# Places of ScalarE and VectorE steps in the mixer stage of a hybrid encoder layer on Trainium2

## Chip, cores and metric

One core of one Trainium2 chip runs the whole program. The metric is device time in microseconds (us), the median of several executions. The hardware profiler gives one further execution with the start and duration of every instruction. Engines are called PE (TensorE matmul), PEld (its weight load), ACT (ScalarE), DVE (VectorE), POOL (GpSimd) and SP (SyncE); POOL and SP issue transfers here.

## What is computed

One layer of a streaming encoder: a macaron feed-forward block, a mixer with two parallel branches, a second feed-forward block, a final norm. 512 prompt tokens and 8 x 16 sample tokens go through it, 640 columns in all. The change concerns the mixer:

```python
def conformer_conv_branch(glu_in, conv_buf, w_dw, b_dw, ln_g, ln_b, w_pw):
    u = glu_in[..., :D_CONV] * jax.nn.sigmoid(glu_in[..., D_CONV:])
    v, new_buf = causal_depthwise_conv(u, conv_buf, w_dw, b_dw)      # width 31
    ...
def mamba2_branch(z, xbc, dt_raw, conv_buf, ssm_state, w_conv, b_conv, dt_bias, a_log, d_skip, norm_g, w_out):
    xbc_c, new_buf = causal_depthwise_conv(xbc, conv_buf, w_conv, b_conv)   # width 4
    xbc_c = jax.nn.silu(xbc_c)
    ...
    dt = jax.nn.softplus(dt_raw.astype(f32) + dt_bias.astype(f32))
    A = -jnp.exp(a_log.astype(f32))
    y, h_fin = ssd_scan(xh, dt, A, Bm, Cm, ssm_state)
    y = (y + d_skip.astype(f32)[:, None] * xh.astype(f32)).reshape(b, L, D_INNER)
    g = (y * jax.nn.silu(z.astype(f32))).reshape(b, L, N_GROUPS, D_INNER // N_GROUPS)
    g = g * lax.rsqrt(jnp.mean(g * g, axis=-1, keepdims=True) + RMS_EPS)
    g = g.reshape(b, L, D_INNER) * norm_g.astype(f32)
    return g.astype(z.dtype) @ w_out, new_buf, h_fin.astype(z.dtype)
```

## The kernel before

**Tiling.** Activations lie transposed, 128 channels by 640 tokens. A matmul in fp32 precision is made of three fp32r products: weights and activations are both split into a high and a low part. A *job* is one block of 128 output channels: 48 matmuls (8 input blocks, three products, two halves of 320 columns), or 24 where the input has 4 blocks. ACT casts a job's raw weights to the high part (`split_hi`, L520), DVE subtracts to get the low part (`split_lo`, L979). There are two weight buffers and two output banks, so job j+2's high part may be written only after job j has ended on PE, and job j+2 starts only once job j's bank has been read out (`evac_done`).

**Order.** Every engine has one queue, and the order in it is the order in which the source writes it; waits are on semaphores, and what is queued behind a wait stands still.

**The mixer.** Four groups (g = 0 to 3) run one after another, each with GJ = 22 jobs, k = 0 to 21. NX = 6 jobs (k = 0 to 5) give x, B and C. Of each, ACT copies the bank into a padded tile and starts the width-4 convolution (`xbc_in`, L762 to L770, five instructions), DVE adds three taps (`conv_xbc`, L1372), ACT applies SiLU (`xbc_silu`, L783) and the D skip (`skip`, L776). k = 6 and 7 are a gate and a value of the conformer branch (J_U0), k = 8 to 11 are z, k = 12 and 13 a second gate and value (J_U1). Five SSD tiles of 128 tokens follow jobs 7 to 11 on PE: in the middle of each of these jobs PE turns x and B (`turn(t)`, L1776 to L1778), at its end it multiplies (`tile(t)`: L1791, L1798, L1804). Tile t needs the decay matrix: ACT takes exponentials of broadcast cumulative sums that POOL's queue fetched from DRAM (`decay(t)`, L799 to L805, `decay_h(t)`, L810), DVE multiplies (`prepare(t)`, L1411). k = 14 to 21 (from J_O) are the output projection, 24 matmuls each, scaled on DVE by the group norm's reciprocal root, which comes from a sum over tokens (L1642), a variance (L995), Ln and Exp on ACT (`inverse_root`, L534 and L536) and three Newton steps on DVE (L1001 to L1005). `sample_state` (L1448) and PE's `sample(b)` (L1836) are the sample tokens' states.

**The width-31 convolution** has 30 taps per channel block on DVE (`conv_glu`, L1344), two blocks c = 0, 1 a group. The table `TAPS` says after which k how many are done; keys from GJ on fall into the next group. Before its first tap ACT copies the block with its halo (`long_conv_in`, L736 to L740) and POOL's queue fetches the sample halo (L449) once the other block's last tap is done.

**Only in group 0** are dt and the cumulative sums made (`dt_stage` on ACT, L709 to L725, and on DVE, L1297 to L1327; `cumulate` on PE, L1751 to L1754). POOL sends the sums to DRAM and fetches them back in broadcast form (`acb`, L464).

## Time and profile before

| | |
|---|---|
| median of 3 runs | 1857.89 us (1857.85 to 1858.5) |
| profiled execution | 1861.42 us, its span 1859.6 us |
| PE busy | 1770.9 us, 95% |
| DVE, ACT, POOL busy | 70%, 47%, 5% |
| mean granted TensorE clock | 0.981 of full speed |
| longest waits of PE, by who ended them | `w_lo` L979 20.3 us in 13 waits; `xa_lo` L1010 9.7 in 1 (at the start); L1791, put down to issue, 9.1 in 4; `h_pr` L1399 4.2 in 3; `ext_b` L764 4.1 in 1; dt's L1322 3.2 in 1 |

The numbers of the profiled execution go with its own time, which lies 3.5 us above the median. "Busy" is the share of the span in which an engine has an instruction in work. The granted clock has two levels in this trace, full (2.4 GHz) and half (1.2 GHz).

### The profile page before, as it was taken

To read this page: it belongs to the slowest core of one execution; us is meant where nothing else is said; L and a number is where in the kernel's file an instruction comes from. 1 tells how busy PE (TensorE), PEld (TensorE's weight loads), DVE (VectorE), ACT (ScalarE), POOL (GpSimd) and SP (SyncE) were. 2 spreads that over 40 slices of the span, in tenths; PEclk is the share of its full clock that TensorE was granted. 3 is DMA by queue.
4 is the path that set the end of the run, shared out by engine and by line. 5 is a ranking of instruction groups with operands and counts; after the bars stand their busy time and mean duration, and the time that the engine had idled before them with its cause. 6 is when DMAs were issued, how large, how long until landed. Compare 5 with 4: busy or idle time off the path is not lost.

```text
span 1859.6 us, 28933 instructions
## 1 busy us (share of the span) xinstructions
PE 1770.9 (95%) x11823; PEld 1712.9 (92%) x11823; DVE 1305.7 (70%) x1626; ACT 870.1 (47%) x1473; POOL 95.4 (5%) x149
## 2 busy tenths in 40 slices
PE   7999999999899999998999899998999999999996
PEld 7999999999888898898889888998999999999995
DVE  6963873776739789879887998775556854863764
ACT  5431441444767357726754773255234432441432
POOL 0000000000011101010201100010000000000000
PEclk9999999999989999999999999999999999999998
DMA  4222212214142344153325423232222212222212
GB/s 157 82 73 84 91 69 91 91 62 142 53 141 77 117 121 137 50 163 100 102 74 148 113 70 125 76 131 68 69 76 73 81 67 91 91 69 91 91 44 81
DMA packets 49714, 173.62 MB, mean 93 GB/s; under 512 B 6800, under 2 KB 6960, under 8 KB 45232
## 3 DMA queue, kind: packets, MB, share of 16 engines
q1 hardware_dynamic: 39024, 137.41, 22.5%
q0 software_dynamic: 10560, 34.38, 6.3%
q8 instruction: 94, 1.54, 0.3%
q14 instruction: 36, 0.29, 0.1%
HBM read 155.56 MB, written 16.20 MB: 92 GB/s over the span
## 4 chain that ended last, share of the span: by engine, by line
PE 78%; DVE 11%; ACT 6%; issue 4%; DMA 1%; ACTq 0%; DVEq 0%; SPq 0%; POOLq 0%
PE ps L1615 48%; PE ps L1676 23%; DVE v L1344 4%; DVE pair L1372 2%; PE ps L1633 2%; DVE w_lo L979 1%; PE ps L1836 1%; ACT w_hi L520 1%; DMA ext_a<-in_halo_a 1%; PE ps L1791 1%; PE ps L1642 1%; ACT acb L802 1%; PE ps L1798 1%; PE ps L1804 1%; PE ps L1825 0%
## 5 line engine op out<-in xcount | busy, mean ns | idle before, releaser
L1615 PE MATMUL ps<-xa_hi,w_hi 128*128 128x320 f32 x1504 | 363.8, 323 | 19.0 <-DVE w_lo L979 11.2
L1615 PE MATMUL ps<-xa_lo,w_hi 128*128 128x320 f32 x1504 | 345.2, 311 | 0.0
L1615 PE MATMUL ps<-xa_hi,w_lo 128*128 128x320 f32 x1504 | 345.2, 311 | 0.0
L520 ACT CAST w_hi<-w_raw 128x1024 fp32r<-128x1024 f32 (+2 forms) x188 | 178.7, 951 | 277.1 <-PE ps L1615 240.2
L1676 PE MATMUL ps<-t_hi,w_hi 128*128 128x320 f32 x952 | 297.0, 312 | 11.5 <-issue 11.5
L1615 PEld LDWEIGHTS ps<-xa_hi,w_hi 128*128 128x128 f32 x1504 | 254.0, 190 | 46.8 <-issue 27.9
L1676 PE MATMUL ps<-t_lo,w_hi 128*128 128x320 f32 x952 | 296.4, 311 | 0.0
L1676 PE MATMUL ps<-t_hi,w_lo 128*128 128x320 f32 x952 | 296.2, 311 | 0.0
L979 DVE TENSOR_TENSOR w_lo<-w_raw,w_hi 128x1024 fp32r<-128x1024 f32 (+2 forms) x188 | 208.2, 1108 | 88.6 <-ACT w_hi L520 86.7
L1615 PEld LDWEIGHTS ps<-xa_lo,w_hi 128*128 128x128 f32 x1504 | 254.1, 190 | 0.0
L1615 PEld LDWEIGHTS ps<-xa_hi,w_lo 128*128 128x128 f32 x1504 | 253.9, 190 | 0.0
L1344 DVE SCALAR_TENSOR_TENSOR v<-ext_a,par,v 128x640 f32<-128x640 f32 x240 | 211.9, 883 | 11.5 <-DMA ext_a<-in_halo_a 5.3
L1676 PEld LDWEIGHTS ps<-t_hi,w_hi 128*128 128x128 f32 x952 | 180.7, 190 | 12.9 <-issue 12.9
L1676 PEld LDWEIGHTS ps<-t_lo,w_hi 128*128 128x128 f32 x952 | 180.7, 190 | 0.0
L1676 PEld LDWEIGHTS ps<-t_hi,w_lo 128*128 128x128 f32 x952 | 180.7, 190 | 0.0
L1615 PE MATMUL ps<-h_hi,w_hi 128*128 128x320 f32 x704 | 160.4, 309 | 0.0
L1615 PE MATMUL ps<-h_hi,w_lo 128*128 128x320 f32 x704 | 160.4, 309 | 0.0
L1615 PE MATMUL ps<-h_lo,w_hi 128*128 128x320 f32 x704 | 160.4, 309 | 0.0
L1231 DVE SCALAR_TENSOR_TENSOR x<-ps,x 128x640 f32<-128x640 f32 x48 | 39.6, 825 | 153.9 <-PE ps L1615 153.5
L1615 PEld LDWEIGHTS ps<-h_lo,w_hi 128*128 128x128 f32 x704 | 117.7, 188 | 0.0
L1615 PEld LDWEIGHTS ps<-h_hi,w_hi 128*128 128x128 f32 x704 | 117.7, 188 | 0.0
L1615 PEld LDWEIGHTS ps<-h_hi,w_lo 128*128 128x128 f32 x704 | 117.7, 188 | 0.0
(264 smaller groups left out, 2619.9 us busy)
## 6 DMA issues: line engine op xcount, KB each, us to landing
w_raw<-in_w_mix SPq DMA_DIRECT2D x56, 512.0 KB, 3.8
raw_b<-in_w_sp SPq DMA_DIRECT2D x18, 1024.0 KB, 4.8
w_raw<-in_w_sp SPq DMA_DIRECT2D x16, 1024.0 KB, 4.8
w_raw<-in_w_down SPq DMA_DIRECT2D x32, 512.0 KB, 3.7
w_raw<-in_w_tail SPq DMA_DIRECT2D x32, 512.0 KB, 3.7
w_raw<-in_w_gu SPq DMA_DIRECT2D x20, 512.0 KB, 3.8
acb<-cum_dram POOLq DMA_DIRECT2D x20, 512.0 KB, 7.3
w_raw<-in_w_ssm SPq DMA_DIRECT2D x32, 256.0 KB, 2.7
```

The lines of the kernel that those rows point to most:

```text
L520: nc.scalar.copy(hi, w_raw[:, b, 0:width]).then_inc(hi_done, 1)
L802: nc.scalar.activation(acb[:, s, j], acb[:, s, j], ACT.Relu, scale=-1.0, bias=tokg[:, 1, t, j:j + 1]).then_inc(dec_step, 1)
L979: nc.vector.tensor_tensor(lo, w_raw[:, b, 0:width], hi.bitcast(F32), ALU.subtract).then_inc(lo_done, 1)
L1231: nc.vector.scalar_tensor_tensor(xc, job_out(b), 0.5, xc, ALU.mult, ALU.add).then_inc(evac_done[b], 1)
L1344: nc.vector.scalar_tensor_tensor(out, ext_a[:, :, j:j + TS], par[:, g, w0 + j:w0 + j + 1], out, ALU.mult, ALU.add).then_inc(conva_ready[c] ...
L1372: nc.vector.scalar_tensor_tensor(out, ext_b[:, s, :, j:j + TS], param(w0 + j), out, ALU.mult, ALU.add).then_inc(tap_b if j < taps - 1 else ...
L1615: last = nc.tensor.matmul(psj[:, b, u, 0:TH], w[:, cols], act_in[:, k, u * TH:(u + 1) * TH], start=(k == 0 and n == 0), stop=(k == chunks ...
L1633: last = nc.tensor.matmul(psj[:, b, u, 0:TH], w[:, b, cols], act_in[:, k, u * TH:(u + 1) * TH], start=(k == 0 and n == 0), stop=(k == chun ...
L1642: last = nc.tensor.matmul(pab[:, u, 0:TH], const[:, ONES], acc[:, u * TH:(u + 1) * TH], start=True, stop=True)
L1676: last = nc.tensor.matmul(ps[:, sp_set(n) + BANK[q], 0:TH], w[:, k * P:(k + 1) * P], t[:, X_OF[q], k * TH:(k + 1) * TH], start=(first and ...
L1791: last = nc.tensor.matmul(pc[e * PD:(e + 1) * PD, c * P:(c + 1) * P], xdt[:, hh * PD:(hh + 1) * PD], mdec[:, hh], start=True, stop=True)
L1798: last = nc.tensor.matmul(pd[:, c * P:(c + 1) * P], h_pr[:, c * P:(c + 1) * P], bc[:, 1, cols], start=True, stop=True)
```

## The change

Five orders change, and the numbers of taps. No instruction is made larger or smaller.

- `inverse_root` of the group norm stands before `next_hi(J_O)` on ACT. On DVE the low split for job 16 stands right behind the read-out of job 14 and no longer behind the sum, sample state and tap that follow it.
- In groups 1 to 3, the halo copies of the previous group's block c = 1 (`long_conv_in(1, g - 1)`) stand behind the high split of job 3 and no longer ahead of it.
- In groups 1 to 3, `tokg`'s copy, `decay(0)` and `decay_h(0)` stand behind `skip(2)` in k = 4 and no longer behind the gate's sigmoid in k = 6.
- In group 0, `dt_stage` on ACT stands behind `xbc_in`, `xbc_silu` and `skip` of its k; on DVE dt's first sum (k = 2) is done at k = 0. `cumulate` on PE and the copies behind it are at k = 6, not 5.
- Taps of c = 0 in the SSD tiles: 4, 3, 3, 3 for 5, 4, 4, 4; block J_O loses its tap; the last job of the group has 2 for 1, the next group's k = 0 has 6 for 4, k = 1 has 3 for 1. Taps of c = 1: 5 for 4 at k = 2, 5 for 6 at 7.5.

```diff
-TAPS = ({8.5: 5, 9.5: 4, 10.5: 4, 11.5: 4} | {k: 1 for k in range(J_O, GJ)} | {GJ: 4, GJ + 1: 1},
-        {GJ + 2: 4, GJ + 3: 4, GJ + 4: 4, GJ + 5: 5, GJ + 6: 7, GJ + 7.5: 6})
+TAPS = ({8.5: 4, 9.5: 3, 10.5: 3, 11.5: 3} | {k: 1 for k in range(J_O + 1, GJ - 1)} | {GJ - 1: 2, GJ: 6, GJ + 1: 3},
+        {GJ + 2: 5, GJ + 3: 4, GJ + 4: 4, GJ + 5: 5, GJ + 6: 7, GJ + 7.5: 5})
...
-                if k == 5:
+                if k == NX:
                     act.wait_ge(cum_mm, 1)
...
+                def scales():
+                    nc.scalar.copy(tokg[:].rearrange("p a t h -> p (a t) h"),
...
                     if k > 3 or not dt_stage:
                         next_hi(k)
-                    if dt_stage:
-                        dt_stage(k)
+                    if k == 2 and g:
+                        long_conv_in(1, g - 1)
                     xbc_in(k)
...
-                    if k == 1 and g:
-                        long_conv_in(1, g - 1)
+                    if dt_stage:
+                        dt_stage(k)
+                    elif k == NX - 2:
+                        scales()
+                        decay(0)
+                        decay_h(0)
...
                 next_hi(J_U1 + 1)
+                inverse_root(N_GROUP + g, 2 + g)
                 next_hi(J_O)
-                inverse_root(N_GROUP + g, 2 + g)
                 next_hi(J_O + 1)
...
-                    if k > 3 or carried:
+                    if (k > 3 or carried) and k != J_O + 1:
                         split_lo(*at(k + 1), KM * P if k + 1 < J_O or k + 1 == GJ else GC * P)
...
-                    else:
+                    elif k != 2:
                         dt_stage(k)
+                    if not carried and k == 0:
+                        dt_stage(2)
...
+                            if c == 0:
+                                split_lo(*at(k + 2), GC * P)
                             evacuated(k)
...
-                        if k == 5 and first:
+                        if k == NX and first:
                             cumulate()
```

ACT in group 0, k = 1 to 3. `xs<-pair` is a SiLU, `pair<-ps` to `new_b<-ext_b` are one `xbc_in`, `dts` are dt's steps.

```order
 L783 ACT_TABLE_LOAD
+L783 ACTIVATE xs<-pair 128x640
+L762 ACTIVATE pair<-ps,parg 128x640
+L764 COPY ext_b<-ps 128x40x16
+L766 COPY ext_b<-halo_b 128x8x3
+L769 COPY ext_b<-ext_b 128x31x3
+L770 COPY new_b<-ext_b 128x27
 L783 ACTIVATE xs<-pair 128x640
 L709 ACTIVATE dts<-dts 128x160
```

The whole `xbc_in` of job 2 and the SiLU of job 1 now stand ahead of dt's first step on ACT.

ACT in groups 1 to 3, k = 4 to 5. The first `CAST` behind these rows is the high part of job 6.

```order
+L783 ACTIVATE xs<-pair 128x640
+L776 ACTIVATE y<-xs,parg 128x640
+L836 COPY tokg<-tok 128x120
+L799 ACT_TABLE_LOAD
+L799 ACTIVATE el<-acb 128x8
+L802 ACTIVATE acb<-acb,tokg 128x128 x8
+L805 ACTIVATE acb<-acb 128x1024
+L810 ACTIVATE ach<-ach 128x512
+L520 CAST w_hi<-w_raw 128x1024
```

Before, the cast followed the `skip` (L776) directly. Two table loads a group come on top, since the SiLUs on both sides need another table.

DVE in group 1 from the norm's variance on, before and then after (line numbers are each kernel's own). `w_lo` ahead of `rstd<-pair` is job 15's, the next one job 16's.

```order
L1448 TENSOR_TENSOR z<-z,ps 128x512
L979 TENSOR_TENSOR w_lo<-w_raw,w_hi 128x512
L1001 SCALAR_TENSOR_TENSOR rstd<-pair 128x640
L1003 TENSOR_TENSOR rstd<-rstd,pair 128x640
L1005 SCALAR_TENSOR_TENSOR rstd<-rstd,pair 128x640
L1509 TENSOR_TENSOR y<-ps,rstd 128x640
L1512 TENSOR_TENSOR yb<-yb,y 128x640
L1448 TENSOR_TENSOR z<-z,ps 128x512
L1344 SCALAR_TENSOR_TENSOR v<-ext_a,par,v 128x640
L979 TENSOR_TENSOR w_lo<-w_raw,w_hi 128x512
```

```order
L986 TENSOR_TENSOR w_lo<-w_raw,w_hi 128x512
L1008 SCALAR_TENSOR_TENSOR rstd<-pair 128x640
L1010 TENSOR_TENSOR rstd<-rstd,pair 128x640
L1012 SCALAR_TENSOR_TENSOR rstd<-rstd,pair 128x640
L1518 TENSOR_TENSOR y<-ps,rstd 128x640
L986 TENSOR_TENSOR w_lo<-w_raw,w_hi 128x512
L1523 TENSOR_TENSOR yb<-yb,y 128x640
```

Job 16's low part has moved ahead of three instructions, and one tap there is gone.

## Rows read from the trace of the kernel before

**Rows 1.** Waits of PE over the span: in all, times, longest.

```profile
PE ps L1615 <- DVE w_lo L979: 20.3, 13, 3.9
```

**Rows 2.** Timeline of PE, group 0: start us, us, instruction, [idle before, releaser].

```profile
500.37 0.87 PE L1615 MATMUL ps<-xa_hi,w_hi 128*128 128x320 f32 x2 [4.07 <-ACT ext_b L764]
...
512.15 0.41 PE L1751 MATMUL ps<-dts,const 128*128 128x32 f32 x2 [3.15 <-DVE dts L1322]
...
546.22 1.10 PE L1791 MATMUL ps<-mdec,xdt 128*64 128x128 f32 x16 [2.96 <-issue]
```

**Rows 3.** Timeline of ACT, group 0.

```profile
493.90 0.74 ACT L783 ACTIVATE xs<-pair 128x640 f32<-128x640 f32 x1
496.75 0.34 ACT L709 ACTIVATE dts<-dts 128x160 f32<-128x160 f32 x1 [2.11 <-DVE dts L1301]
...
508.86 1.02 ACT L520 CAST w_hi<-w_raw 128x1024 fp32r<-128x1024 f32 x1
```

**Rows 4.** POOL's timeline in group 0, and landing of line L464's transfers.

```profile
522.78 0.94 POOL L464 DMA_DIRECT2D acb<-cum_dram  x1 [2.08 <-DMA cum_dram<-cum_sb]
...
DMA to landing us min/median/max: 4.8/7.3/8.7
```

**Rows 5.** Chain of work that ended last: start us, us, what.

```profile
518.92 9.49 PE ps L1615 x48
...
549.51 4.31 PE ps L1615 x24
...
789.63 5.32 PE ps L1615 x24
795.82 3.52 PE ps L1615 x24
...
899.87 4.87 PE ps L1615 x24
```

**Rows 6.** Timeline of PE, group 1 and (898.67) group 2.

```profile
670.81 0.55 PE L1615 MATMUL ps<-xa_hi,w_hi 128*128 128x320 f32 x2 [1.76 <-DVE w_lo L979]
...
711.16 1.61 PE L1791 MATMUL ps<-mdec,xdt 128*64 128x128 f32 x16 [2.03 <-issue]
...
789.63 0.56 PE L1615 MATMUL ps<-gn_hi,w_hi 128*128 128x320 f32 x2 [2.48 <-DVE w_lo L979]
...
898.67 0.66 PE L1776 MATMUL ps<-const,xs 128*128 128x128 f32 x4 [1.87 <-DVE h_pr L1399]
```

**Rows 7.** Timeline of ACT, group 1, k = 2 to 7.

```profile
668.46 1.03 ACT L520 CAST w_hi<-w_raw 128x1024 fp32r<-128x1024 f32 x1
...
685.48 0.89 ACT L762 ACTIVATE pair<-ps,parg 128x640 f32<-128x640 f32 x1 [3.09 <-PE ps L1615]
...
688.68 1.04 ACT L520 CAST w_hi<-w_raw 128x1024 fp32r<-128x1024 f32 x1
...
704.71 1.28 ACT L799 ACT_TABLE_LOAD   x1
...
710.23 0.25 ACT L832 COPY btok<-ps 128x128 f32<-128x128 f32 x1
```

**Rows 8.** Timeline of DVE, group 1, k = 5 to 7.

```profile
691.53 1.22 DVE L979 TENSOR_TENSOR w_lo<-w_raw,w_hi 128x1024 fp32r<-128x1024 f32 x1
692.66 4.56 DVE L1344 SCALAR_TENSOR_TENSOR v<-ext_a,par,v 128x640 f32<-128x640 f32 x5
...
709.84 1.22 DVE L1411 TENSOR_TENSOR mdec<-acb,cbm 128x1024 f32<-128x1024 f32 x1 [0.59 <-ACT acb L805]
```

**Rows 9.** Timelines of DVE and ACT, group 1, k = 13 to 15.

```profile
777.62 0.82 DVE L995 TENSOR_SCALAR pair<-ps 128x640 f32<-128x640 f32 x1 [0.42 <-PE ps L1642]
...
783.32 0.83 DVE L1001 SCALAR_TENSOR_TENSOR rstd<-pair 128x640 f32<-128x640 f32 x1 [2.34 <-ACT pair L536]
...
788.89 0.69 DVE L979 TENSOR_TENSOR w_lo<-w_raw,w_hi 128x512 fp32r<-128x512 f32 x1
...
782.47 0.74 ACT L536 ACTIVATE pair<-pair 128x640 f32<-128x640 f32 x1
```

More of the change, by code:

```diff
@@ L832, in btok_out @@
                     nc.scalar.copy(btok[:], pb[:, 0:NS]).then_inc(btok_ready, 1)
+                def scales():
+                    nc.scalar.copy(tokg[:].rearrange("p a t h -> p (a t) h"),
+                                   tok[:].rearrange("p a t h -> p (a t) h")[:, :, bass.ds(g * HG, HG)]
+                                   ).then_inc(tokg_ready, 1)
+                    act.wait_ge(tokg_ready, g + 1)
                 if not dt_stage:
@@ L857, in group @@
                     dt_stage(NX)
-                nc.scalar.copy(tokg[:].rearrange("p a t h -> p (a t) h"),
-                               tok[:].rearrange("p a t h -> p (a t) h")[:, :, bass.ds(g * HG, HG)]
-                               ).then_inc(tokg_ready, 1)
-                act.wait_ge(tokg_ready, g + 1)
-                if dt_stage:
+                    scales()
                     act.wait_ge(cum_out, 16)
@@ L866, in group @@
                 next_hi(J_U0 + 1)
-                decay(0)
-                decay_h(0)
+                if dt_stage:
+                    decay(0)
+                    decay_h(0)
                 btok_out(0)
@@ L1515, in group @@
                                                     ALU.mult).then_inc(evac_done[b], 1)
+                            if c == 0:
+                                split_lo(*at(k + 2), GC * P)
                         if c < NB - 2:
```

## Prediction, made before the changed kernel ran

> **What bounds the kernel now.** I read the busy shares first (PE 95%), then who ended PE's waits, then the timelines around each wait. PE is the bound, so only its idle time and the time it spends at half clock can be won. The biggest entry is the low weight parts, 20.3 us in 13 waits [rows 1]. In the mixer the timelines place the waits like this. Group 0 stands still before job 4 for 4.07 us (the bank of job 2 has not been copied out), before `cumulate` for 3.15 and before tile 0 for 2.96 [rows 2]. Each of groups 1 to 3 has the same pattern: 1.76 before job 3, 2.03 before tile 0, up to 1.87 in the middle of job 9 (turn 2), and 2.48 before job 16 [rows 6]. An idle stretch often costs twice, since the granted clock falls to half behind it. Job 16 takes 5.32 us where the next job of 24 matmuls takes 3.52; a half job behind turn 2 of group 2 takes 4.87, and one behind tile 0 of group 0 takes 4.31; job 5 behind `cumulate` takes 9.49 where 48 matmuls at full clock take 7.04 [rows 5]. Everything outside the mixer keeps its order, and I cost it at nothing.
>
> I work in the profiled execution's own time (1861.42 us, span 1859.6, 1.8 us around it) and subtract the sum from the median shown, 1857.89, which lies 3.5 lower.
>
> **1. The norm's root and job 16's split (groups 1 to 3).** The variance ends at 777.62 + 0.82 = 778.44, but Exp starts only at 782.47, because Ln stood behind job 15's cast, which waits for job 13, and paid its table load after that [rows 9]. Now Ln's table load waits for nothing and lies ahead of the variance. Ln runs at 778.45 (0.74), a table load (1.28 [rows 7]) and Exp (0.74) end at 781.2. Job 15's cast and low part (about 0.65 each) follow, so DVE's first Newton step starts at 782.4, 0.9 earlier. Three steps and the read-out of job 14 at 0.83 each give 785.7 [rows 9], and job 16's low part, now next, ends at 786.4. Before it started at 788.89 [rows 9]. PE is through with the work ahead of job 16 at 787.15, which is 789.63 less 2.48 [rows 6] (0.2 earlier by the spacing of later jobs, as each sample product overlaps). So the 2.48 wait goes. Job 15 may start 0.3 later, since its cast now stands behind the root. The half clock behind the wait goes too: 5.32 - 3.52 = 1.80 [rows 5]. **Gain 2.48 + 1.80 - 0.3 = 4.0 a group, 12.0 in three.** Late next is job 17's low part, whose cast stands behind job 14's two neighbours and 16 small sample copies on ACT; by the same spacings it is ready at about 791.3, when PE is done with job 16 and its sample product, so up to 0.5 may be lost. The Newton steps overwrite a tile that still leaves for DRAM; they start 0.9 earlier than before, and that transfer could become the wait; bounds 0 and 0.9. Group 0 has the same pattern without a marked half clock; I put its gain at 1.6, the nearest row being its own wait of that kind in [rows 1], bounds 0.5 and 2.5.
>
> **2. Halo copies behind job 3's cast.** The cast at 668.46 [rows 7] moves ahead of 2.5 us of copies, and job 3 starts without its 1.76 wait. But DVE is the bound in k = 2 to 6: from 670.8 on it has no pause, and every job there is released by a low part that comes at the end of a k. What counts is when DVE starts its taps of k = 2. These need the copies, which end at about 669.5, and the sample halo. Before they began 1.1 later, behind the low part; now they begin 1.1 earlier but are 5 for 4, and a tap costs 4.56 / 5 = 0.91 [rows 8]. **Gain 0.2 a group; the 1.76 wait reappears before job 4.** Bounds: -1 (the halo, fetched once the two added taps of k = 1 are done, comes late) and +0.4. I take 0.2.
>
> **3. First decay in k = 4 (groups 1 to 3): a loss.** It takes 710.23 - 704.71 = 5.52 us with its table load [rows 7], plus 0.3 for `tokg`. Behind it now stands job 6's cast. Job 4's `xbc_in`, a SiLU and a skip take 688.68 - 685.48 = 3.20 [rows 7], so the cast starts at 685.25 + 3.20 + 5.82 = 694.3 and ends at 695.3, and DVE's low part for job 6 waits for that; before it ran at 691.53 [rows 8]. DVE stands still for 3.8 us, PE before job 6 for about 4.3, and this is on the path, as DVE is the bound from there to tile 0: 711.16 - 691.53 = 19.6 us of work in a row [rows 6, 8]. What comes back is the 0.59 that the decay product waited for its exponentials [rows 8]. **Loss 3.8 - 0.6 = 3.2 a group, 9.6 in three.** PE's half clock after the 4.3 us wait (1.7 us) is hidden, because job 7 waits for DVE anyway; if it lasts twice as long, about 1 us shows. Bounds of the loss: 2.0 (all of the 2.03 before tile 0 [rows 6] comes back, 3.8 - 1.8) and 5.5 (half clock shows in full, 3.8 + 1.7).
> On the table loads first the row: 1.28 us, and the decay's first exponential starts right behind it, so two more a group are in the sum at 1.28 where they are on the path (one of them; the SiLU's stands in ACT's slack). The Trainium skill, page "ScalarE: Activation LUTs", section "What ACT_TABLE_LOAD costs", puts a switch at 2.66 us, the load and a drain of 1.38. By that rule the loss would be 1.4 larger a group, 4.1 in all, and the sum 15.1 for 19.2, a time of 1842.8. The rows show no such drain, so I leave it out.
>
> **4. Fewer taps in the SSD tiles.** From tile 0 to turn 2, DVE does 6 + 5 taps around the halo fetch; now 5 + 4, that is 1.8 us less on the chain that ended the wait of 1.87 [rows 6]. **Gain 1.7 in group 1, 1.7 + 1.35 (4.87 - 3.52, the half clock [rows 5]) in group 2, 1.6 in group 3: 6.4.** Bounds 3 and 7. The taps that move to the last job, k = 0 and k = 1 lie in DVE's pauses there and cost nothing; if the pause in k = 1 is shorter than I read, 0.9 a group. The tap-free tiles behind turn 2 were bound by PE and gain nothing.
>
> **5. dt's steps in group 0.** ACT waited for dt's first sum until 496.75 and copied job 2's bank only then [rows 3]. Now the sum is made at k = 0, and `xbc_in` of job 2 follows the SiLU of 493.90 directly, at 494.6; the bank is free at 496.1, when job 3 ends (500.37 - 4.07 = 496.3 [rows 2]). So the 4.07 goes. From 496.75 to 508.86 ACT works without a pause, 12.1 us; the same pieces in the new order need one table load less, 10.8, so job 5's cast starts at 494.6 + 10.8 = 505.4 for 508.86 [rows 3] and its low part ends at 507.6. Job 4 ends at 496.3 + 7.04 = 503.4: **a new wait of 4.2 before job 5** takes the place of the old one. `cumulate` then finds dt ready, so 3.15 goes [rows 2]. Job 5, with 1.7 of half clock, ends at 507.6 + 7.05 + 1.7 = 516.4; `cumulate` took 518.92 - 512.15 = 6.8, mostly at half clock [rows 2, 5]; at full clock 4.5. Job 6 then takes 7.04 to 9.49 [rows 5]. With 4.5 and 9.1 it ends at 530, for 535.3 before; with 6.8 and 9.49 at 532.7. ACT is free then, while before it was 2.7 late with the gate's sigmoid. Sigmoid, job 8's cast, table load and exponentials bring the decay to 536.9, PE ends job 7 at 530 + 8.3 = 538.3, and tile 0 starts there for 546.22 [rows 2]. The exponentials also need the broadcast sums: `cumulate` ends at 521, the copies at 522.6, the transfer to DRAM takes some 2.9 (2.08 of it POOL's wait), and the fetch 7.3 (up to 8.7) [rows 4]: 532.8 to 534.2, just when ACT wants them, at 533.0. **Gain 7.9, bounds 4.5 and 8.5**; plus 0.8 (4.31 - 3.52 [rows 5]) as no wait stands before tile 0. I take the upper part of the range since both halves of the chain, PE's and ACT's, meet there.
>
> **The sum:** 12.0 + 1.6 + 0.6 - 9.6 + 6.4 + 8.7 = 19.7, less 0.5 for job 17: 19.2. 1861.4 - 19.2 = 1842.2 profiled, 1857.9 - 19.2 = **1838.7**.
>
> **Rivals.**
> - *The decay costs its upper bound and the clock takes the rest.* Part 3 at 5.5 a group (16.5), part 5 at 5, part 4 at 3: 13.6 - 16.5 + 0.6 + 3 + 5 - 0.5 = 5.2 to about 12 with one of the three at its middle. Time 1846 to 1853. For it: the clock stayed at half through `cumulate` and into job 5. Against: nothing, except that DVE hides one half clock.
> - *The root's order brings nothing*, because job 15's cast behind the root, or job 17's behind the sample copies, becomes the wait: 12 less, 1850.7. Against: PE has 3.9 to 4.4 us a job there, and DVE's work a job is shorter.
> - *Slower:* the decay ahead of job 6's cast. PE waits 4.3 us, then again before job 7 and tile 0, and stays at half clock over all three. The point is reached when the loss is over 11 us a group for my 3.2, that is, 15 us at half clock on the path (7.5) on top of 3.8: 1857.9 - 28.8 + 34 = 1863. For it: a row of waits in group 0 did hold the clock low from tile to tile. Against: between these waits PE works through whole jobs of 7 us, unlike in `cumulate`.
> - *Nothing to speak of:* the waits of groups 1 to 3 only change place (parts 1 to 4 sum to 0) and group 0 gives 3: 1855.
> - *Better:* the decay's wait is nearly regained at tile 0 (2.0 a group), part 5 at its bound: 1834.
>
> **Chances.** Forecast and its near bounds, 1834 to 1844: 0.62. First rival 0.14, second 0.08, nothing 0.06, slower 0.05, better than 1834 0.05. For 8 in 10 I go from 1832 to 1850. About 0.2%, 3.7 us, is what a measurement can tell from no change. Faster than 1854.2: 0.88, same: 0.07, slower: 0.05.
>
> **What would show it.** Right: no wait of PE before job 16 and none before job 4 of group 0; a wait of about 4 us before job 6 in groups 1 to 3, ended by `w_lo`, with ACT's decay ahead of the cast; one of about 4 before job 5 in group 0; tile 0 of group 0 at about 538; turn 2 without a wait. Wrong: a wait before job 15 or 17 of over 0.5 us, half clock in job 7 or behind tile 0, the halo or the broadcast sums as the releaser of DVE or ACT for over 1 us.

## The result, and the profile after

The changed kernel takes **1851.36 us** (median of 7 runs, 1850.12 to 1851.85). The kernel before, run beside it, takes 1857.89 (1855.83 to 1858.5). The ratio is 0.9966, 95% interval 0.9954 to 0.9977: faster by 6.5 us, where 19.2 were forecast, and outside the range of 1832 to 1850.

The profiled execution took 1850.33 us, its span 1848.4. A second profile of the kernel before (the first experiment) has a span of 1854.4, not 1859.6. The two differ by 5.2 us with no change of the kernel: the trace that the prediction was read from lies 3.5 above the median, the second one 1.2 below its own. The 6.0 us between 1854.4 and 1848.4 agree with the 6.5 of the medians. Where stretches are compared below, the kernel before stands with this second trace.

Waits of PE over the span of the changed kernel (in all, times, longest), which answer to [rows 1]:

```profile
PE ps L1628 <- DVE w_lo L986: 28.5, 13, 4.3
PE ps L1804 <- issue: 5.8, 7, 3.0
PE ps L1817 <- ACT xtl L819: 3.6, 3, 1.2
```

The waits for low weight parts did not shrink from 20.3, they grew to 28.5. The timeline of PE says where (start us, us, instruction, [idle before, releaser]); it answers to [rows 2, 6]:

```profile
507.21 0.90 PE L1628 MATMUL ps<-xa_hi,w_hi 128*128 128x320 f32 x2 [4.13 <-DVE w_lo L986]
...
539.39 1.31 PE L1804 MATMUL ps<-mdec,xdt 128*64 128x128 f32 x16 [3.01 <-issue]
...
669.05 0.56 PE L1628 MATMUL ps<-xa_hi,w_hi 128*128 128x320 f32 x2 [1.86 <-DVE w_lo L986]
...
689.27 0.90 PE L1628 MATMUL ps<-xa_hi,w_hi 128*128 128x320 f32 x2 [4.34 <-DVE w_lo L986]
...
707.15 1.09 PE L1804 MATMUL ps<-mdec,xdt 128*64 128x128 f32 x16 [0.76 <-issue]
...
856.16 0.90 PE L1628 MATMUL ps<-xa_hi,w_hi 128*128 128x320 f32 x2 [4.06 <-DVE w_lo L986]
...
887.61 1.10 PE L1817 MATMUL ps<-xtl,btok 128*128 128x512 f32 x2 [1.20 <-ACT xtl L819]
```

In group 0, the 4.07 before job 4 and the 3.15 before `cumulate` are gone, 4.13 stands before job 5, and the wait before tile 0 is still there (3.01 for 2.96). In group 1, 1.86 stands before job 4, 4.34 before job 6, and no wait stands before job 16 or at turn 2. New is the last row, 1.20 in tile 1 for `xtl`, in each of groups 1 to 3. DVE's timeline shows what is behind these (687.99 is the low part of job 6 in group 1, 854.88 the same in group 2, 776.99 that of job 15, 882.90 the second decay product; they answer to [rows 8, 9]):

```profile
687.99 1.22 DVE L986 TENSOR_TENSOR w_lo<-w_raw,w_hi 128x1024 fp32r<-128x1024 f32 x1 [5.37 <-ACT w_hi L520]
...
776.99 0.69 DVE L986 TENSOR_TENSOR w_lo<-w_raw,w_hi 128x512 fp32r<-128x512 f32 x1 [1.44 <-ACT w_hi L520]
...
854.88 1.23 DVE L986 TENSOR_TENSOR w_lo<-w_raw,w_hi 128x1024 fp32r<-128x1024 f32 x1 [3.94 <-ACT w_hi L520]
...
882.90 1.23 DVE L1418 TENSOR_TENSOR mdec<-acb,cbm 128x1024 f32<-128x1024 f32 x1 [1.22 <-ACT acb L805]
```

ACT's timeline of group 2 (848.30 to 853.30 is the first decay in its new place, 853.82 job 6's cast, 877.78 the load ahead of the second decay; it answers to [rows 7]):

```profile
848.30 1.28 ACT L799 ACT_TABLE_LOAD   x1
849.59 0.22 ACT L799 ACTIVATE el<-acb 128x8 f32<-128x8 f32 x1
...
853.30 0.61 ACT L810 ACTIVATE ach<-ach 128x512 f32<-128x512 f32 x1
853.82 1.03 ACT L520 CAST w_hi<-w_raw 128x1024 fp32r<-128x1024 f32 x1
...
876.71 1.05 ACT L520 CAST w_hi<-w_raw 128x1024 fp32r<-128x1024 f32 x1
877.78 1.28 ACT L799 ACT_TABLE_LOAD   x1
879.07 0.22 ACT L799 ACTIVATE el<-acb 128x8 f32<-128x8 f32 x1
```

**Where the time went.** All kernels here issue the same 11,823 matmuls, from group 1 on in one order, so two traces can be laid side by side by the number of the matmul. What the changed kernel gains (-) or loses (+) against the second trace of the kernel before, worked out from the start times of the same matmuls, and the forecast for the same stretch:

| stretch | measured, us | forecast, us |
|---|---|---|
| up to the mixer | +1.1 | 0 |
| group 0 to tile 0 (part 5 without the clock behind tile 0) | -6.2 | -7.9 |
| rest of group 0: clock behind tile 0 (0.8 of part 5), root | -2.0 | -2.4 |
| groups 1 to 3, job 3 to tile 0 (parts 2, 3) | +4.9 +3.3 +3.7 = +12.0 | +9.0 |
| groups 1 to 3, tile 0 to turn 2 (part 4) | -0.7 -0.5 -0.7 = -1.8 | -6.4 |
| groups 1 to 3, turn 2 to job 17 (part 1) | -4.2 -4.0 -2.6 = -10.8 | -11.5 |
| behind the mixer | +1.9 | 0 |
| sum (before rounding) | -6.0 | -19.2 |

Three stretches are worked out for the experiments too, in us for groups 1 / 2 / 3. The first runs from matmul 4240 of the program (in job 2; 1063 more for each group) to tile 0 (4509), the second from tile 0 to just behind turn 2 (4640), the third from just ahead of the norm's sum over tokens (4960) to the middle of job 17 (5070):

```
kernel                 job 2 to tile 0         tile 0 to turn 2        job 14 to job 17
before, 1st trace      45.51 / 45.51 / 45.51   19.90 / 20.23 / 19.68   22.61 / 22.58 / 22.57
before, 2nd trace      45.50 / 45.51 / 45.60   19.75 / 19.57 / 19.77   22.61 / 22.45 / 21.06
halo copies alone      44.39 / 44.41 / 44.39   19.76 / 19.66 / 19.93   22.60 / 22.59 / 22.59
taps alone             46.42 / 46.43 / 46.44   19.29 / 18.94 / 19.09   20.27 / 20.27 / 20.27
decay alone            49.04 / 49.06 / 49.08   19.70 / 19.55 / 19.88   22.59 / 21.05 / 21.06
decay and taps         50.29 / 50.30 / 50.31   19.10 / 19.09 / 19.08   20.27 / 20.27 / 20.27
root alone             45.62 / 45.61 / 45.51   19.55 / 19.62 / 19.61   19.24 / 19.24 / 19.24
after                  50.38 / 48.85 / 49.33   19.10 / 19.09 / 19.09   18.44 / 18.45 / 18.45
after, decay in place  45.43 / 45.41 / 45.42   19.13 / 19.12 / 18.01   18.44 / 18.44 / 18.44
after, decay split     49.87 / 48.35 / 49.87   17.90 / 17.89 / 17.75   18.45 / 18.45 / 18.44
after, decay late      46.09 / 44.84 / 46.11   17.85 / 17.76 / 18.00   18.45 / 18.44 / 18.45
late and gate first    46.07 / 46.11 / 44.84   18.02 / 18.02 / 17.83   18.45 / 18.44 / 18.44
```

### The profile page after: what moved, and what is told of

The parts are those of the page before. It is cut to its first block, busy times and chain, and to the rows that moved or that the text cites. A ratio compares the mean times of both kernels' runs of the same rounds, so it can differ in the third digit from the quotient of the medians.

```text
span 1848.4 us, 28936 instructions
## 1 busy us (share of the span) xinstructions
PE 1766.7 (96%) x11823; PEld 1712.3 (93%) x11823; DVE 1306.7 (71%) x1626; ACT 877.6 (47%) x1479; POOL 95.1 (5%) x149
## 4 chain that ended last, share of the span: by engine, by line
PE 85%; ACT 6%; DVE 5%; issue 3%; DMA 0%; ACTq 0%; DVEq 0%; SPq 0%; POOLq 0%
PE ps L1628 54%; PE ps L1689 23%; PE ps L1646 2%; PE ps L1849 1%; DVE w_lo L986 1%; DVE v L1351 1%; PE ps L1804 1%; PE ps L1817 1%; ACT w_hi L520 1%; ACT acb L802 1%; PE ps L1655 1%; DVE pair L1379 1%; PE ps L1811 1%; PE ps L1838 0%; PE ps L1789 0%
## 5 line engine op out<-in xcount | busy, mean ns | idle before, releaser
L1628 PE MATMUL ps<-xa_hi,w_hi 128*128 128x320 f32 x1504 | 365.4, 325 | 29.2 <-DVE w_lo L986 28.5
L1689 PE MATMUL ps<-t_hi,w_hi 128*128 128x320 f32 x952 | 297.0, 312 | 11.5 <-issue 11.5
```

The costliest lines, as they stand in the source:

```text
L1628: last = nc.tensor.matmul(psj[:, b, u, 0:TH], w[:, cols], act_in[:, k, u * TH:(u + 1) * TH], start=(k == 0 and n == 0), stop=(k == chunks ...
L1689: last = nc.tensor.matmul(ps[:, sp_set(n) + BANK[q], 0:TH], w[:, k * P:(k + 1) * P], t[:, X_OF[q], k * TH:(k + 1) * TH], start=(first and ...
```

## Experiments

Each kernel was timed in five rounds beside the kernel before, and each ratio is to that one's runs. "Forecast" means the term of the prediction.

### The kernel before once more

Edit: none. 

> The kernel before, unchanged. Its profiled execution took 3.5 us more than its median. If that was chance in where the half-clock stretches fell, this run's trace has fewer or cheaper such stretches and its own time is near 1858. If the profile itself costs something, its own time is again near 1861.4. The timed ratio is 1.000 either way.

Measured: 1857.57 us, ratio 1.0000 (0.9992 to 1.0009), span 1854.4. No wait of PE in its trace differs from the first one's by over 0.6 us in all (the low parts read 20.2 in 13); what differs is where PE stood at half clock: the first trace lost 1.7 us more ahead of the mixer, 2.1 in group 2 and 1.4 in group 3. So a difference of 1 to 2 us between two traces here, in one stretch, can be such a half clock alone.

### The first decay back in its old place

```diff
-                    elif k == NX - 2:
-                        scales()
-                        decay(0)
-                        decay_h(0)
...
+                scales()
...
-                if dt_stage:
-                    decay(0)
-                    decay_h(0)
+                decay(0)
+                decay_h(0)
```

> The changed kernel with only the first decay of groups 1 to 3 (and the copy ahead of it) back in its old place behind the gate's sigmoid. Theory of the late cast: the decay ahead of job 6's cast costs 3.2 us a group, as predicted, plus 1.3 in the SSD tiles, where the exponentials' table has to be loaded again for the second decay; this kernel is 12 to 14 us faster than the changed one, about 1838. Prediction as written: 9.6 us faster, about 1841.7. Rival (the loss lies in group 0 or in how the clock falls, and the decay cost what it gave back): within 3 us of 1851.4.

Measured: **1836.39 us** (1834.39 to 1837.76), ratio 0.9888 (0.9874 to 0.9901). The move of the decay costs the changed kernel 15.0 us, more than half as much again as the forecast's 9.6. (Each of the two kernels against the kernel before beside it, 21.0 and 6.5 faster, gives 14.5.) Without it the change would have given 21 us.

### The decay's move alone, on the kernel before

Edit: the first diff in reverse, on the kernel before. 

> The kernel before with only the first decay moved to k = 4. Theory of the late cast: slower than before by 9 to 13 us, 1867 to 1871, with a wait of about 4 us before job 6 in each of groups 1 to 3 and one of about 1.2 before the state product of tile 1. Rival (the decay's move is hidden by the 2.0 us before tile 0 and by the low clock): within 4 us of 1857.9.

Measured: 1867.21 us (1866.76 to 1867.83), ratio 1.0055 (1.0042 to 1.0068), so +9.8 us. DVE's timeline in group 2 shows the wait that the forecast put at 3.8:

```profile
866.61 1.22 DVE L987 TENSOR_TENSOR w_lo<-w_raw,w_hi 128x1024 fp32r<-128x1024 f32 x1 [3.94 <-ACT w_hi L520]
```

Job 2 to tile 0 grows by 3.5 in each group, for a forecast of 3.2. So the step was sized rightly for this kernel. It costs more in the changed one, and the traces show where. There, group 2 pays 3.4 (48.85 less 45.41), but group 1 pays 5.0, and its wait on DVE is 5.37 instead of 3.94. Group 3 pays 3.9. The halo copies and the added tap have put a wait of 1.86 before job 4. The clock granted to PE behind it, in group 1 (669) and for comparison group 2 (837), from windows of the changed kernel (us, PE busy, PEclk, DMA share, GB/s):

```profile
669.00:674.00 5.00, 4.95 (x23) 0.66 0.34 108
837.00:842.00 5.00, 4.54 (x31) 1.00 0.30 105
```

Where job 4 runs partly at half clock, its bank is full about 1.4 us later, `xbc_in` waits for that bank, and now the decay and job 6's cast stand behind `xbc_in`. With the decay in its old place the time to tile 0 is the same in all groups (45.43 / 45.41 / 45.42), though that trace has half clock in job 4 of each: DVE hides it, and the decay's move lays it open.

Group 3's own 0.5 has another cause. Before its job 4 PE waits 2.33 for 1.86, because DVE's taps of k = 2 waited for the sample halo's transfer (in group 2 they waited 1.31 for ACT's copies):

```profile
996.44 4.57 DVE L1351 SCALAR_TENSOR_TENSOR v<-ext_a,par,v 128x640 f32<-128x640 f32 x5 [1.80 <-DMA ext_a<-in_halo_a]
```

### The root's order alone

```diff
+                inverse_root(N_GROUP + g, 2 + g)
                 next_hi(J_O)
-                inverse_root(N_GROUP + g, 2 + g)
...
-                    if k > 3 or carried:
+                    if (k > 3 or carried) and k != J_O + 1:
...
+                            if c == 0:
+                                split_lo(*at(k + 2), GC * P)
```

> The kernel before with only the group norm's root and job 16's low part moved. Prediction: 12.0 + 1.6 - 0.5 = 13.1 us faster, about 1844.8; the two traces aligned at PE's matmuls say 4.2 in each of groups 1 to 3 and 2.5 in group 0, 15 in all, 1843. Rival (the removed wait comes back at job 15 or 17): under 5 us faster, above 1853.

Measured: 1846.12 us (1845.24 to 1848.15), ratio 0.9942 (0.9929 to 0.9956), -11.3 for a forecast of 13.1. Job 14 to 17 takes 19.24 in every group, for 22.6 where half clock follows the wait before job 16, and 21.06 in the one group of the second trace where it does not. The wait before job 16 is gone, and none stands before job 15. But in each of groups 1 to 3 a new one of 0.6 stands before job 17. In group 1:

```profile
789.52 0.56 PE L1619 MATMUL ps<-gn_hi,w_hi 128*128 128x320 f32 x2 [0.62 <-DVE w_lo L979]
```

### dt's steps alone

```diff
-                if k == 5:
+                if k == NX:
                     act.wait_ge(cum_mm, 1)
...
-                    if dt_stage:
-                        dt_stage(k)
                     xbc_in(k)
...
+                    if dt_stage:
+                        dt_stage(k)
...
-                        if k == 5 and first:
+                        if k == NX and first:
                             cumulate()
```

and DVE's second step at k = 0. 

> The kernel before with only dt's steps of group 0 in their new places. Prediction: 8.7 us faster, about 1849. Theory from the traces (the sums' way to DRAM took 4.8 us for 2.1, and ACT stands still for it ahead of the gate's table load): 6 us faster, about 1851.5, with ACT waiting about 3 us ahead of the skip that follows the exponentials of dt. Rival (new wait before job 5 takes all): within 2 us of 1857.5.

Measured: 1850.62 us (1848.95 to 1852.92), ratio 0.9967 (0.9955 to 0.9979), -6.3 for a forecast of 8.7, as the theory read from the traces had it. In the trace 6.3 lie ahead of tile 0, and ACT waits 3.14 for the sums' way to DRAM ahead of the skip.

### The table of taps alone

Edit: the two lines of `TAPS`. 

> The kernel before with only the new tap numbers. Prediction: 6.4 us faster, 1851, as the wait before turn 2 goes in groups 1 to 3. Rival (one tap more in k = 2 ahead of the bound low parts costs 0.9 a group in full, since the copies still stand ahead of job 3's cast): 3 to 4 us faster, 1853.5. Second rival (the wait only moves to ACT's copies): no change.

Measured: 1852.1 us (1850.32 to 1853.39), ratio 0.9970 (0.9958 to 0.9981), -4.8. The forecast was 6.4, and the gain does not come from where the forecast had it. From tile 0 to turn 2 only some 0.6 a group is gained, for 1.7, though the wait at turn 2 is gone. Job 2 to tile 0 loses 0.9: that is the fifth tap in k = 2, in a stretch that DVE bounds, as the first rival said. Job 14 to 17 gains 2.2 to 2.3 in two groups and 0.8 in the third: the tap of k = 14 is gone from DVE's way to job 16's low part. I had not counted that at all, and it is the same wait that part 1 removes. In the changed kernel it adds only 0.8 (19.24 less 18.44), by removing the wait before job 17 that the root's order alone leaves.

Where the rest of the 1.7 went shows in the second trace of the kernel before. Behind tile 0 of group 1 it has half clock, behind that of group 2 it has not (PE busy, PEclk, DMA share, GB/s):

```profile
709.00:713.00 4.00, 3.54 (x19) 0.61 0.44 160
877.00:881.00 4.00, 2.90 (x24) 1.00 0.44 152
```

Tile 0 to turn 2 takes 19.75 and 19.57 all the same: DVE ended the stretch and hid the half clock. With two taps fewer, and half clock behind tile 0 in all three groups of that trace, PE's own work at that clock ends it, at 18.9 to 19.3.

### decay_h behind the gate

```diff
                         decay(0)
-                        decay_h(0)
...
                     decay(0)
-                    decay_h(0)
+                decay_h(0)
```

This leaves the early decay where it is, but the last function that ACT runs before tile 0 is an exponential again. Its table load falls in ACT's pause there, and the second decay needs none. 

> The changed kernel with only the second exponential of tile 0 (decay_h(0), one instruction of 0.6 us) back behind the gate. It makes the exponentials' table be loaded in ACT's pause there and not ahead of the second decay. Theory of the table load: the waits of 1.2 us before the state product of tile 1 go in groups 1 to 3, turn 2 comes about 0.9 us earlier still, and job 6's cast 0.5 us earlier: 4 to 6 us faster than the changed kernel, 1846. Rival (the table load was hidden, only the half microsecond in k = 4 counts): 1.5 us faster, 1850.

Measured: 1844.89 us (1842.38 to 1847.44), ratio 0.9935 (0.9921 to 0.9949), 6.5 below the changed kernel. ACT's timeline, group 1:

```profile
701.19 1.28 ACT L810 ACT_TABLE_LOAD   x1
702.48 0.63 ACT L810 ACTIVATE ach<-ach 128x512 f32<-128x512 f32 x1
706.16 0.27 ACT L832 COPY btok<-ps 128x128 f32<-128x128 f32 x1 [3.04 <-DVE cbm L1413]
...
710.15 1.05 ACT L520 CAST w_hi<-w_raw 128x1024 fp32r<-128x1024 f32 x1
711.10 0.22 ACT L799 ACTIVATE el<-acb 128x8 f32<-128x8 f32 x1
```

The load and `ach` stand ahead of a pause of 3.04, and the second decay (711.10) follows the cast without a load. Tile 0 to turn 2 falls from 19.10 to 17.90, 1.2 or 1.3 a group, and job 2 to tile 0 by the 0.5 of `ach` in groups 1 and 2. **That table load, 1.28 us on ACT between two tiles, is shown to cost about 1.2 a group.** Both traces have the same number of table loads, 60, for 54 before: what counts is where the load stands. The spans differ by 5.4. Of this 3.7 lie between tile 0 and turn 2 and 0.5 from job 2 to tile 0 (group 3 has half clock in job 4 here and loses 0.5); the rest lies outside groups 1 to 3. Against the kernel before beside each, the medians give 5.5 for the 6.5.

### Decay and taps on the kernel before

Edit: the decay's move and the table of taps together, on the kernel before. 

> The kernel before with two of the changes alone: the first decay of groups 1 to 3 in k = 4, and the new table of taps. Apart they measured +9.8 and -4.8 us. Theory of the added table load: behind the early decay another function of ACT runs last, so the second decay needs a table load of 1.28 us of its own, and it stands between tile 0 and turn 2, just where the missing taps bring DVE through earlier. The taps' gain is then mostly eaten: 1865 to 1867 us, and the trace shows DVE waiting for ACT's exponentials ahead of its second decay product. Rival, the two changes don't touch each other: the effects add, 1857 + 9.8 - 4.8 = 1862 us.

Measured: 1864.5 us (1863.43 to 1865.54), ratio 1.0038 (1.0026 to 1.0051), +6.7. Adding the two single effects gives +5.0, and the difference of 1.7 is inside the intervals. By the times alone neither theory is settled. Of the 1.7 the traces show some 1.0, and not where the first theory has it: job 2 to tile 0 is 0.3 a group longer than with the two effects added (50.30 for 49.96). The trace does show the wait that the first theory names (DVE, group 2):

```profile
894.09 1.22 DVE L1419 TENSOR_TENSOR mdec<-acb,cbm 128x1024 f32<-128x1024 f32 x1 [1.23 <-ACT acb L805]
```

Yet tile 0 to turn 2 is no longer than with the taps alone (19.1 and 19.1). Both are held at 19.1, by different things. With the decay in its old place PE waits about 2 us before tile 0 and runs job 8 partly at half clock behind it. With the decay early that wait is short and the clock full, but the table load holds DVE. PE's clock in the 4 us behind tile 0 of group 1, first with the decay in its old place, then in the changed kernel:

```profile
700.00:704.00 4.00, 3.42 (x21) 0.72 0.26 90
```
```profile
707.00:711.00 4.00, 3.85 (x31) 1.00 0.35 119
```

Only where both are absent does the stretch fall to 17.8, 1.8 to 1.9 below the kernel before, where the forecast wanted 1.7: with the decay split, with it late, and in group 3 with the decay in place (18.01). In that group the clock stayed up behind tile 0, with the same wait of 2.03 before it:

```profile
1027.00:1031.00 4.00, 3.46 (x28) 1.00 0.26 85
```

### The decay late

```diff
+                    if k == NX - 1 and not dt_stage:
+                        scales()
+                        decay(0)
                     xbc_in(k)
+                    if k == NX - 1 and not dt_stage:
+                        next_hi(J_U0)
...
-                    elif k == NX - 2:
-                        scales()
-                        decay(0)
-                        decay_h(0)
```

and `decay_h(0)` behind the gate. 

> The changed kernel with the first decay of groups 1 to 3 behind the cast of job 6 (k = 5) in ACT's pause there, decay_h(0) behind the gate and job 7's cast ahead of the SiLU. Theory of the late cast: no wait of 4 us before job 6, none for the exponentials before tile 0; at least as fast as the kernel with the old decay (1836.4), by 0.6 us a group at best: 1834 to 1836. Rival (anything that leaves less than a microsecond of slack to xbc_in or to job 7's cast costs as much as the old wait): 1838 to 1842.

Measured: **1834.91 us** (1831.74 to 1836.02), ratio 0.9876 (0.9862 to 0.9891), faster than both kernels. ACT's timeline, group 1:

```profile
682.83 1.03 ACT L520 CAST w_hi<-w_raw 128x1024 fp32r<-128x1024 f32 x1
683.77 0.29 ACT L836 COPY tokg<-tok 128x120 f32<-128x120 f32 x1
684.08 1.28 ACT L799 ACT_TABLE_LOAD   x1
...
690.90 1.04 ACT L520 CAST w_hi<-w_raw 128x1024 fp32r<-128x1024 f32 x1
```

Job 6's cast goes first, so DVE's low part for it has no wait, and job 7's cast still comes in time. It is 10.0 below the kernel with `decay_h` alone behind the gate, which still has `decay(0)` ahead of that cast (the late decay also moves job 7's cast ahead of the SiLU). So it was the decay's place ahead of job 6's cast that cost, not an early decay as such. Half clock in job 4 still shows, 1.3 in groups 1 and 3 (46.1 for 44.84). Against the decay in its old place the gain is 1.5 us, and the two intervals overlap.

### The gate first in group 0

```diff
                     scales()
-                    act.wait_ge(cum_out, 16)
-                skip(0)
+                else:
+                    skip(0)
                 glu_gate(J_U0)
                 next_hi(J_U0 + 1)
                 if dt_stage:
+                    act.wait_ge(cum_out, 16)
+                    skip(0)
```

> The changed kernel; in group 0 the gate's sigmoid and job 8's cast stand ahead of ScalarE's wait for the running sums and of skip(0). Theory that ScalarE's queue behind that wait ends the chain to tile 0: sigmoid, cast and one table load (3 us) leave it, tile 0 starts 2 to 3 us earlier, 1848.5 to 1849.5. Rival, the transfer of the sums to DRAM and back ends it: the exponentials' input landed at 534.25 us, 0.7 us after ScalarE was ready for it, so nothing or at most 0.5 us is gained, 1851 us.

Measured: 1850.45 us (1849.01 to 1852.78), ratio 0.9963 (0.995 to 0.9975), the same as the changed kernel within its interval. In the changed kernel and here, ACT's first exponential:

```profile
534.25 0.22 ACT L799 ACTIVATE el<-acb 128x8 f32<-128x8 f32 x1 [0.69 <-DMA acb<-cum_dram]
```
```profile
533.28 0.22 ACT L799 ACTIVATE el<-acb 128x8 f32<-128x8 f32 x1 [1.16 <-DMA acb<-cum_dram]
```

In both traces ACT is ready and waits, so the fetch of the sums ends the chain, by 0.7 and 1.2 us. The edit did not clear ACT's queue, though. The gate's sigmoid could not start before PE had ended job 6 (its table load stands at 527.16, behind 3.28 of waiting for PE), and the skip still followed it. Counted from the copy of the sums, ACT was ready 11.1 us later in both kernels; only the fetch landed 0.5 later. So this run shows that the new order gains nothing, not what a free ACT would gain.

### The halo copies alone

Edit: `long_conv_in(1, g - 1)` ahead of `xbc_in(2)`. 

> The kernel before with the halo copies of groups 1 to 3 behind job 3's cast alone, 2.5 us of ScalarE a group. Forecast -0.2 a group, 1856.5 to 1857 us: the wait of 1.76 before job 3 goes and one of 1.8 before job 4 comes. Rival: the halo lands late for the taps of k = 2, +1 a group, 1860 us. Second rival: the wait before job 3 goes and nothing comes back, -1.8 a group, 1852 us.

Measured: 1855.54 us (1852.58 to 1858.15), ratio 0.9989 (0.9980 to 0.9998), -2.3. Job 2 to tile 0 is shorter by 1.1 in every group, and no half clock follows in job 4: no wait stands before job 3 and one of 0.93 before job 4. My expectation was wrong here: the 0.2 a group was the forecast for the copies and the added tap together. It is 1.1 for the copies less 0.9 for the tap, and both numbers now stand measured (1.1, and 0.9 with the taps alone).

### Late decay and gate first

Edit: both on the changed kernel. 

> The changed kernel with the late decay (first decay's exponentials in k = 5 behind the cast of job 6, the rest behind the gate) and the gate first in group 0. If ScalarE's queue ends group 0's chain: 1832 us, 2 to 3 below the late decay alone (1834.9). If the transfer of the sums ends it: 1834.5 us.

Measured: 1834.53 us (1832.24 to 1837.02), ratio 0.9877 (0.9863 to 0.9890), the same as the late decay alone, as the theory of the transfer has it, with the same limit: the gate first does not make ACT ready earlier.

## Why the prediction was wrong

The sign was right, and the waits stood mostly where they were foretold: before jobs 4 and 6 of groups 1 to 3, before job 5 of group 0, none before job 16. The sum was out by 12.7 us, and several terms failed in the same direction. The step that failed by its mechanism is part 4, with the table load that part 3 left out: the time that DVE no longer needs between tile 0 and turn 2 was taken as PE's gain. The other terms were mis-sized.

**Part 1, right in its mechanism, its size in part by luck.** Variance at 772.80, DVE's Newton step at 777.60, no wait before job 16. 10.8 for 11.5. But 0.8 a group of it is the tap missing from k = 14, which the forecast did not know. The root's order alone gives 3.4 a group for 4.0, as job 17 then waits 0.6 in each group, where the forecast allowed 0.5 in all. With the tap gone job 17 does not wait.

**Part 2, right**: 1.1 less 0.9. What was not seen is the wait's second effect. It moved to job 4 and at times takes the clock down there. In group 3 the halo came late by 0.5, within the bound of -1.

**Part 3, mis-sized.** The working (DVE 3.8, PE 4.3, less 0.6) was right to 0.3 a group for the kernel before. Two things were missing. The step read ACT's times of job 4 from [rows 7], where the move of part 2 was not yet in; with job 4 at half clock in group 1 the wait became 5.37. That is about 1.5 in one group of this trace (the late halo of group 3 is another 0.5); in the decay split, which has it in two groups, job 2 to tile 0 reads 49.87 twice and 48.35 once. And the step counted two added table loads, "one of them" on the path and the other in the SiLU's slack. The second decay's was not among them. The load that stood ahead of the first decay behind the gate did not go with it. The next user of that function pays for the switch: the load at 877.78 with DVE waiting 1.22. The move costs 15.0 by the medians for 9.6. The traces (decay in place against the changed kernel) show 12.3 up to tile 0 and 1.1 from tile 0 to turn 2 of group 3, 13.4 in the groups; in groups 1 and 2 the second load's cost is hidden there by the half clock that goes (next part). The spans differ by 16.0: the other 2.6 lie ahead of the mixer (1.9) and behind it (0.8), where both kernels have one order, and I count them as chance.

On the drain of 1.38 that the Trainium skill adds to a table load (page "ScalarE: Activation LUTs", "What ACT_TABLE_LOAD costs"), the rows of the changed kernel agree with those of before: the load starts at 877.78, takes 1.28, and the exponential starts at 879.07. The rule would have brought the forecast nearer to the measured loss, by a cost that no row here shows.

**Part 4, the step that failed most.** 1.8 for 6.4. It took DVE's shorter work as PE's gain, on the ground of the wait of 1.87 at turn 2 [rows 6]. The wait went as foretold, and the two taps' time was there (19.75 falls to 17.8 in two experiments), but the stretch has another limit at 19.1: half clock in job 8 with the decay in its old place, the second decay's table load with the early one. The taps alone meet the first limit, 0.6 a group for 1.7; the changed kernel meets the second. The half clock at 899.87 [rows 5] was chance too: the second trace of before has its own in other places.

**The sum of the parts.** The single experiments sum to -14.9 us (-11.3 -6.3 -4.8 -2.3 +9.8), the whole gives -6.5. The traces show two overlaps. The root's order and the taps remove one wait and the half clock behind it: 3.4 and 2.3 a group alone, 4.2 together (18.44 for 22.6), so up to 1.5 a group stands twice in the sum. And job 2 to tile 0 loses 12.0 over the three groups, for 9.8 by the single edits. Tile 0 to turn 2 has no overlap, 1.8 for the whole as for the taps alone. The rest of the 8.4 is not resolved; five differences of medians, each uncertain by some 2 us, are added there.

**Part 5, mis-sized.** 6.2 to tile 0 for 7.9, and little of the 0.8 behind it. The waits before job 4 and `cumulate` went as worked out, and job 5's wait is 4.13 for 4.2. But the two halves of the chain did not meet. PE ended job 7 at 536.4 for 538.3, at full clock, and then waited 3.01; the half over the sums was late. They were copied out at 523.4 for 522.6, their way to DRAM took 5.6 for 2.9 (POOL's wait in it 4.82 for 2.08), the fetch 5.2 for 7.3. The exponentials started at 534.25 for 533.0 and tile 0 at 539.39 for 538.3. Of POOL's queue:

```profile
523.68 0.53 POOL L435 DMA_DIRECT2D cum_dram<-cum_sb  x1 [64.98 <-ACT tok L721]
529.02 0.94 POOL L464 DMA_DIRECT2D acb<-cum_dram  x1 [4.82 <-DMA cum_dram<-cum_sb]
```

That is 1.1. Another 0.6 is the trace's own start: PE was 0.58 ahead at the mixer before any of this. Of the 0.8 for full clock behind tile 0 only 0.3 came, since 3.01 of wait still stand before it and the clock granted from 538 to 544 is 0.72.

**Outside the mixer, costed at nothing.** The trace gives +1.1 ahead of it and +1.9 behind. Behind it, a window of the changed kernel:

```profile
1260.00:1267.00 7.00, 5.37 (x20) 0.53 0.23 75
```

This is half clock behind a wait of 3.72 that both kernels have. Other variants have less of it there (the late decay gains 1.8 against the changed kernel in just that stretch). I take it for chance, like the rest, but no run settles that.

**The chances.** The time fell into the place of the second rival, "the root's order brings nothing", for none of its reasons, and near the top of the first, which had the decay at its upper bound (it came to 5.0 a group for a bound of 5.5), part 4 at 3 (1.8) and part 5 at 5 (6.2). As I read it, the range was too narrow because these bounds were treated as independent. Of the signs named for being wrong, three came: half clock behind tile 0 (of group 0), the sums' transfer as ACT's releaser (3.10 ahead of the skip), and the halo as DVE's (1.80 in group 3).

## What to carry to other kernels

When an activation with its own table moves, look at the place of every table load behind it in the queue, not only at those around its new place. An instruction that used to find the table loaded may now stand behind the load. Before a step is moved behind something that another engine ends, ask what has been hiding delays of that something: a bank that was ready early enough became the releaser. And before an engine's shorter work is booked as gain, look for what that engine's bound has hidden, half clock above all: the stretch falls only to the next limit. Where two edits work on one stretch, cost them together against that limit.

## What the hardware showed

**A small transfer took longer beside large ones.** The 80 KB of running sums took 2.0 us from issue to landing in the kernel before and 4.7 in the changed one. All seven traces of kernels with dt's old order have 2.0, the seven with the new one 4.7 to 5.1. The window of the changed kernel in which it travels, and the one of before (us, busy time of PE, PEld, DVE, ACT, POOL, then PEclk, DMA share, GB/s):

```profile
524.00:529.00 5.00, 5.00 (x37) 5.00 (x36) 0.00 (x0) 1.85 (x4) 0.21 (x1) 1.00 0.89 323
```
```profile
520.00:523.00 3.00, 3.00 (x13) 3.00 (x12) 0.00 (x0) 0.00 (x0) 0.75 (x2) 0.50 0.12 27
```

The move put it beside the loads of the sample states, which SP's timeline of the changed kernel shows at the same time:

```profile
523.29 0.91 SPq L357 DMA_DIRECT2D pair<-in_h_sample  x2
524.24 0.94 SPq L357 DMA_DIRECT2D ext_b<-in_h_sample  x2
```

No run moved those away, so that this is the cause is argued, not shown.

**Half clock moves between executions.** Two profiles of one kernel differ by 5.2 us of span, with no wait that differs by over 0.6. Terms of 1 to 2 us that rest on a half clock read in one trace have that uncertainty, each.
